# Experts sorted by token count, 24 small ones four at a time, and rows by one-hot products in the last 12 steps of a mixture-of-experts kernel

## What is computed

```
t = x.reshape(-1, D)                                    # 264 tokens, D = 1024
scores = sigmoid(t @ w_router)                          # 64 experts
biased = scores + router_bias                           # 8 groups of 8: the 4 best groups stay,
_, eidx = top_k(where(emask > 0, biased, -inf), 8)      # of them each token takes 8 experts
w = take_along_axis(scores, eidx);  w = w / sum(w) * 2.5
h = silu(t @ w_gate[e]) * (t @ w_up[e])                 # 1024 -> 256, for each expert
routed = (h * comb[..., e]) @ w_down[e]                 # 256 -> 1024, summed over experts
shared = (silu(t @ ws_gate) * (t @ ws_up)) @ ws_down    # one more expert for all tokens
x = layer_norm(ALPHA * x + routed + shared)
```

## Time and profile before

| | |
|---|---|
| median of the runs | 824.3 us (3 runs, 824.23 to 824.31) |
| the profiled execution: its time | 824.56 us |
| its span | 822.8 us |
| TensorE busy | 805.0 us, 98% |
| VectorE busy | 465.1 us, 57% |
| ScalarE busy | 166.1 us, 20% |
| GpSimd busy | 93.1 us, 11% |
| bytes moved by DMA | 262.15 MB |

### The profile page before, as it was taken

One profiled execution on the slowest core, in us unless ns is written; L12 is line 12 of the kernel. 1 busy time (PEld: TensorE's weight loads), 2 busy tenths in 40 slices (PEclk: granted clock), 3 DMA queues, 4 the chain that ended last, 5 costly groups with the idle time before them and its releaser, 6 DMA issues.

```text
span 822.8 us, 11931 instructions
## 1 busy us (share of the span) xinstructions
PE 805.0 (98%) x4283; PEld 500.9 (61%) x4283; DVE 465.1 (57%) x1178; ACT 166.1 (20%) x275; POOL 93.1 (11%) x105
## 2 busy tenths in 40 slices
PE   9999999999999999999999999999999999999995
PEld 7876788888788888544545445454544445445443
DVE  6989899999741367533434334443444434334356
ACT  2210112111221005321211212121121212112126
POOL 1119700000010002100000000000000000000021
PEclk9999999999999999999999999999999999999998
DMA  9432344445489946699999999999999999999981
GB/s 333 151 128 103 122 139 149 155 154 115 142 321 417 414 182 249 219 397 416 423 423 420 423 425 424 422 427 420 425 425 423 424 426 424 420 424 419 419 351 53
DMA packets 45372, 262.15 MB, mean 319 GB/s; under 512 B 9928, under 2 KB 10696, under 8 KB 26256
## 3 DMA queue, kind: packets, MB, share of 16 engines
q1 hardware_dynamic: 40720, 252.88, 76.6%
q0 software_dynamic: 4608, 8.66, 2.8%
HBM read 267.10 MB, written 2.53 MB: 328 GB/s over the span
## 4 chain that ended last, share of the span: by engine, by line
PE 83%; DMA 9%; SPq 6%; DVE 1%; issue 1%; ACT 1%; ACTq 0%; DVEq 0%
PE banks L1263 35%; PE banks L1474 21%; PE banks L1518 10%; PE banks L1435 6%; DMA high<-w_gu 5%; SPq L464 4%; DMA ring<-w_gu 4%; PE banks L1410 3%; SPq L472 2%; PE banks L1364 1%; PE banks L1278 1%; PE banks L1495 1%; PE banks L1290 1%; PE banks L1440 1%; DMA ring<-w_front 1%
## 5 line engine op out<-in xcount | busy, mean ns | idle before, releaser
L1474 PE MATMUL banks<-high,low 128*64 128x512 f32 x848 | 230.1, 593 | 0.9 <-DMA high<-w_gu 0.9
L1263 PE MATMUL banks<-xT,ring 128*128 128x264 f32 x768 | 176.3, 389 | 0.3 <-DMA ring<-w_front 0.3
L1170 DVE TENSOR_TENSOR cgb<-cgb,banks 128x264 f32<-128x264 f32 x248 | 89.8, 423 | 132.1 <-PE banks L1435 131.9
L1263 PEld LDWEIGHTS banks<-xT,ring 128*128 128x128 f32 x768 | 144.5, 190 | 30.4 <-issue 5.5
L1474 PEld LDWEIGHTS banks<-high,low 128*64 128x64 f32 x848 | 73.6, 137 | 138.6 <-issue 135.1
L1222 DVE SCALAR_TENSOR_TENSOR y_pair<-banks,sml,y_pair 128x1024 fp32r<-128x1024 f32 x31 | 39.8, 1284 | 121.8 <-ACT y_pair L725 121.8
L1474 PE MATMUL banks<-ring,low 128*64 128x512 f32 x176 | 77.6, 593 | 3.0 <-DMA ring<-w_gu 3.0
L562 POOL DMA_INDIRECT low<-x_rows_dram,idx x32 | 31.9, 997 | 423.5 <-DVE idx L1114 403.0
L1435 PEld LDWEIGHTS banks<-sw,y_pair 128*128 128x128 f32 x496 | 63.0, 188 | 24.9 <-issue 23.5
L1518 PE MATMUL banks<-high,mu 128*64 128x512 f32 x336 | 77.0, 599 | 0.7 <-ACT mu L705 0.7
L1435 PE MATMUL banks<-sw,y_pair 128*128 128x264 f32 x496 | 71.1, 293 | 0.0
(11 more groups left out here) (300 smaller groups left out, 859.9 us busy)
## 6 DMA issues: line engine op xcount, KB each, us to landing
high<-w_gu SPq DMA_DIRECT2D x35, 2048.0 KB, 24.0
high<-w_dn SPq DMA_DIRECT2D x40, 1024.0 KB, 21.9
ring<-w_front SPq DMA_DIRECT2D x78, 512.0 KB, 3.2
high<-w_gu SPq DMA_DIRECT2D x34, 1024.0 KB, 11.5
ring<-w_gu SPq DMA_DIRECT2D x7, 2048.0 KB, 28.8
us<-w_dn SPq DMA_DIRECT2D x11, 1024.0 KB, 21.8
ring<-w_gu SPq DMA_DIRECT2D x8, 1024.0 KB, 12.0
bgb<-w_dn SPq DMA_DIRECT2D x6, 1024.0 KB, 21.4
```

The costliest lines, as they stand in the source:

```text
L1170: dve.tensor_tensor(acc[:, n], acc[:, n], psum[:, bank, 0:T], ALU.add).then_inc(added, 1)
L1263: ins = pe.matmul(psum[:, 6 + n % 2, 0:T], ring[:, n % RING, k], rhs[:, k], start=(k == 0), stop=(k == KC - 1))
L1474: ins = pe.matmul(psum[SL * j:SL * j + SL, GU_BANK, :], xg[:, k, SL * j:SL * j + SL], gu[slots[j]][:, k], start=(k == 0), stop=(k == KC - 1))
```

## The change

It touches the expert part alone.

- **Order.** The first 8 experts keep their places. The other 56 are ranked by their number of tokens, on VectorE and TensorE, in front of and during step 0: a key for each expert, its rank by comparison, a permutation matrix `places`, and products that permute picks and gates (`turn_gates`, `sort_gates`, `count_sorted`, in the gate/up products of step 0). The expert numbers by place go into a tile `order`, from which SP reads each number into a register (`expert`) before it refills.
- **Four at a time.** Places 30 to 61 hold the 24 smallest experts in six groups of four, with pairs of the largest between them. Pairs 13 to 30 are worked off in 12 steps of `(1, 1, 2, 1, 2, 1), (2, 1, 2, 1, 2, 2)` pairs. A step of two pairs has 32 slots for each of its four experts, and its products go to four column parts of 32. It needs both pairs' weights, and both of its refills wait for its own `gu_done` and `dn_done`. There are 26 steps in place of 32.
- **Rows by products.** In the last 12 steps before the final one, `gather_rows` takes the place of the indirect DMA and of `turn`: 16 products of the token rows, which stay in SBUF (`xrow`, now in `xcb`, where `dn[7]` was), with `S32`, an f32 copy of the one-hot matrix that GpSimd makes (`widen`), and 8 small ones for the 8 sample rows. `dn[7]` and its early load go.
- The counts of rounds come from the sorted lists; rounds are added where one of the 24 smallest has more than 32 tokens or another more than 64. The three late refills are no longer in halves. The shared expert's down products move to the first three steps of four.

```diff
+        FIXED = 8
+        MIXED_FROM = 13
+        MIXED = ((1, 1, 2, 1, 2, 1), (2, 1, 2, 1, 2, 2))
+        mixed_pairs, nth = [], MIXED_FROM
+        for n in itertools.chain(*MIXED):
+            mixed_pairs.append(tuple(range(nth, nth + n)))
+            nth += n
...
+        SHARED_AT = {2: (0, 1, 2), 4: (3, 4), 6: (5, 6, 7)}
...
 
-        xrow = [y_flat[:, 0:D], y_flat[:, D:2 * D], y_rest]
+        xcb_flat = xcb[:].rearrange("p k t -> p (k t)")
+        xrow = [xcb_flat[:, 0:D], xcb_flat[:, D:2 * D], y_rest]
+        sample_rows = y_all[:, D + 64 - HC * P:D + 64]
+        S32, = carve(x_rows, (TC, 2 * SL))
...
-        DOWN_PAIRS = ((4, 5), (0, 1), (2, 3), (7, 5), (0, 1), (2, 3))
+        DOWN_PAIRS = ((4, 5), (0, 1), (2, 3))
...
-                sp.wait_ge(x1_scaled, KC)
-                sp.dma_start(dn[7], w_dn[6]).then_inc(dn_in[7], 16)
                 for c in range(TC):
                     sp.wait_ge(xrow_ready, c + 1)
...
+                def expert(place):
+                    return sp.value_load(order[0:1, bass.ds(place, 1)] if not isinstance(place, int) else order[0:1, place:place + 1], min_val=0, max_val=E - 1)
+
+                refill(0, 0, SLOT_PAIRS[0], DOWN_PAIRS[0], [6, 7], halves=True)
+                sp.wait_ge(order_ready, 1)
+                for it in range(1, 1 + PER_TURN):
+                    refill(it, it, SLOT_PAIRS[it % 3], DOWN_PAIRS[it % 3], [2 * it + 6, 2 * it + 7], halves=it < EARLY_HALVES, by_place=True)
+                    if it == 1:
+                        sp.wait_ge(weights_ready, 2)
+                        sp.wait_ge(rows_stored, 16 * TC)
+                        for g in range(2):
+                            sp.dma_start(sample_rows[32 * g:32 * g + NS], x_dram[LP:T, HC * P * g:HC * P * (g + 1)]).then_inc(rows_stored, 16)
                 sp.wait_ge(lists_ready, 1)
-                refills = sp.value_load(rounds[0:1, 1:2], min_val=TURNS - 1, max_val=MOST - 1)
-                for it in range(5):
-
-                    refill(it, SLOT_PAIRS[it % 3], DOWN_PAIRS[(it + 3) % 6] if it else (None, 5), [2 * it + 6, 2 * it + 7], halves=it < EARLY_HALVES)
...
+                after_middle = sp.value_load(rounds[0:1, 1:2], min_val=PLAIN - 2, max_val=MOST - 2)
+                middle = sp.snap(after_middle + 1)
+
+                def later_refill(q, it, step, fill):
+                    places = [(q * (2 * PER_TURN) + (2 * it + 6 + j)) % E for j in range(2)]
+                    fill(q * PER_TURN + it, q * PER_TURN + step, SLOT_PAIRS[it % 3], DOWN_PAIRS[it % 3], places, by_place=True)
+
+                with sp.Fori(0, middle) as q:
+                    for it in range(1 + PER_TURN, 1 + 2 * PER_TURN):
+                        later_refill(q, it, it, refill)
+                for a, pairs in enumerate(mixed_pairs):
+                    for it in pairs:
+                        if it + 3 < PAIRS:
+                            later_refill(after_middle, it, MIXED_FROM + a, last_refill if it + 3 == PAIRS - 1 else refill)
...
+                def widen(step, u):
+                    pool.wait_ge(select_ready, step + 1)
+                    pool.wait_ge(turned, step)
+                    pool.sem_inc(rows_moved, 1)
+                    pool.tensor_copy(S32, S[:, u]).then_inc(widened, 1)
...
+                for a in range(len(mixed_pairs)):
+                    widen(mixed * PER_TURN + (a + 2), a % 2)
...
+                def first_visit():
+                    match_tokens(0, 0)
+                    dve.wait_ge(weights_read, 4)
+                    dve.tensor_copy(gain[:, 0], meta[:, 0, 0:1]).then_inc(gain_ready, 1)
+                    dve.wait_ge(selected, 1)
+                    dve.wait_ge(shifted, 2)
+                    select(0, 4, 2, 3)
+                    dve.wait_ge(sort_products, GATES_SORTED)
+                    do(dve.tensor_scalar(order[0:1], psum[0:1, SORT_BANKS[1], TC * P:TC * P + E], 1.0, -1.0, ALU.mult, ALU.add))
+                    dve.sem_inc(order_ready, 1)
+                    do(dve.tensor_copy(sorted_gates, psum[:, SORT_BANKS[1], 0:TC * P].rearrange("p (c t e) -> p c t e", c=TC, t=2)))
+                    do(dve.tensor_copy(pk, picks))
+                    dve.sem_inc(sort_inputs, 1)
+                    do(dve.tensor_scalar(picks, picks, -1000.0, 1000.0, ALU.mult, ALU.add))
+                    gate_rows(0)
+                    dve.wait_ge(selected, 3)
+                    dve.wait_ge(turned, 1)
+                    dve.wait_ge(sw_ready, 1)
+                    dve.wait_ge(gain_ready, 1)
+                    indices(0, 6, 2)
+                    count_leftovers()
+                    split_rows(0, 0)
+                    split_gates(sorted_gates[:, :, 1, FIXED:E], slice(FIXED, E))
+
...
+                def gather_rows():
+                    def columns(k):
+                        return psum[:, 2 + k // 4, (k % 4) * P:(k % 4) * P + P]
+
+                    for k in range(KC):
+                        for c in range(2):
+                            pe.matmul(columns(k), xrow[c][:, k * P:k * P + P], S32[:, c], start=(k % 4 == 0 and c == 0), stop=False)
+                    for h in range(HC):
+                        for g in range(2):
+                            rows = slice(32 * g, 32 * g + NS)
+                            ins = pe.matmul(columns(HC * g + h), sample_rows[rows, h * P:h * P + P], S32[rows, 2], start=False, stop=(h == HC - 1))
+                    ins.then_inc(turned, 1)
+
+                def turn_gates():
+                    pe.wait_ge(sort_inputs, GATES_READY)
+                    pe.wait_ge(shared_silu, 1)
+                    for c in range(TC):
+                        ins = pe.transpose(psum[:, SORT_BANKS[0], c * P:c * P + P], gates[:, c].rearrange("p t e -> p (t e)"), ident[:])
+                    ins.then_inc(sort_products, 1)
+
+                def sort_gates():
+                    pe.wait_ge(sort_inputs, GATES_COPIED)
+                    pe.wait_ge(sort_inputs, RANKED)
+                    pe.wait_ge(shared_h, FC)
...
                                 pe.wait_ge(gu_last_rows[j], 16)
-                            ins = pe.matmul(psum[SL * j:SL * j + SL, GU_BANK, :], xg[:, k, SL * j:SL * j + SL], gu[slots[j]][:, k],
+                            ins = pe.matmul(psum[size * j:size * j + size, GU_BANK, :], xg[:, k, size * j:size * j + size], gu[s][:, k],
                                             start=(k == 0), stop=(k == KC - 1))
                         if k == HC - 1:
                             ins.then_inc(gu_mid, 1)
-                            if gathers is None:
+                            if last:
                                 pe.wait_ge(y_split, it)
                                 pe.wait_ge(sw_ready, it)
                                 combine(1 - u, before, shared, rows_summed_first=True)
+                        if before is None and k == 1:
+                            turn_gates()
+                        if before is None and k == 4:
+                            sort_gates()
                     ins.then_inc(gu_done, 1)
-
-                    if gathers is None:
+                    if before is None:
+                        count_sorted()
...
+                        if isinstance(before, int) and before == 0:
+                            pe.wait_ge(lists_ready, 1)
                         combine(1 - u, before, shared)
...
+                        if wide is None:
+                            pe.wait_ge(gathered[1 - u], gathers)
+                        else:
+                            pe.wait_ge(widened, wide)
                         if before is not None:
                             banks_added(before, 2, 3)
-                        turn()
-
+                        if wide is None:
+                            turn()
+                        else:
+                            gather_rows()
...
-                visit(turns * PER_TURN + 1, 1, SLOT_PAIRS[1], DOWN_PAIRS[1], turns * 32 + 16, 4, before=turns * (PER_TURN * KC))
+                        visit(q * PER_TURN + k, k % 2, [k], [q * 32 + 16 * (k // 3 + 1)], before=q * (PER_TURN * KC) + KC * (k - 1),
+                              ahead=((q * PER_TURN + (k + 2)) % PAIRS * 2, 2), gathers=q * 48 + 16 * ((k + 1) // 2 + 1))
+                pe.wait_ge(rows_stored, 16 * (TC + 2))
+
+                def mixed_place(a):
+                    pairs = mixed_pairs[a] if a < len(mixed_pairs) else (PAIRS - 1 + a - len(mixed_pairs),)
+                    return within((mixed * (2 * PER_TURN) + (2 + 2 * (pairs[0] - MIXED_FROM))) % E, len(pairs)), 2 * len(pairs)
+
+                for a, pairs in enumerate(mixed_pairs):
+                    loaded = [mixed * 32 + 16 * ((1 + r - MIXED_FROM) // 3 + 1) for r in pairs]
+                    visit(mixed * PER_TURN + (a + 1), (a + 1) % 2, pairs, loaded, before=mixed * (PER_TURN * KC) + KC * a, ahead=mixed_place(a + 2),
+                          wide=mixed * PER_TURN + (a + 2), shared=SHARED_AT.get(a, ()))
```

(57 more changed lines are left out.)

325 lines of the change are left out of this document (210 added, 115 removed).

## The result

The changed kernel takes 826.9 us (median of 8 runs, 825.7 to 828.1) against 824.2 for the kernel before on the same chip: ratio 1.003, 95% interval 1.0022 to 1.0039, so 1.8 to 3.2 us slower. A repeat on another occasion gave 827.0 (10 runs), ratio 1.003 again. The forecast was 823.4, slightly faster; the time lies inside the range given and on the other side of no change.

A forecast was written before the change was run, and what follows sets the result against it. The end was taken as pair 30's landing plus TensorE's work after it, so DMA bytes and idle time bound. Landing -10.4, after it +9.5, together -0.9: 823.7 profiled, 823.4 as median; 8 in 10 within 818.8 to 828.0.

The forecast's parts named there:

- landing of pair 30: Arrival of pair 30's gate/up weights, the last that TensorE waits for: 10.4 us earlier than 782.22, near 772.
- row products: Token rows made by products on TensorE in late steps: 5.3 us in place of 1.06 for turning.
- The gathers: In the weight stream, 1173 rows no longer gathered: -12.0 us, between 12.8 by q0's packet time and 11.3 by bytes.
- The early `w_dn`: Expert 6's down weights, loaded after step 0's down products in the full stream instead of early: +1.8 us (1.3 to 2.5).
- The front: Sort in front and in step 0, mostly hidden: net +0.3 us on the stream (-0.7 to +3).
- Loading whole instead of by halves: Three late pairs load whole, at 424 rather than 419 GB/s: -0.5 us (0 to -1).
- its +7.6: TensorE's work after pair 30's landing, now in a quad: 18.4 us where 10.8 was, +7.6 (6.5 to 8.7).
- The clock: Last quad after its wait: an idle engine is put at half rate, penalty certain, +1.9 us.
- Four tiles side by side: Gate/up of four experts takes 6.9 us; the rival, only two tiles at a time, gives 841 us, chance 5%.
- the stream has no hole in the quads: Weight loads during quads: 12 us still queued when the rest of the refills comes, so the stream never runs dry.
- The sort delays step 0: Slower rival, 12%: extra VectorE work before step 1's `sw` idles the DMA; ten slower operations give 826 to 827.5.
- The last quad is not slowed: Faster rival, 20%: clock stays up or recovers at once, row products at 0.213, gathers worth packet time: 819 us.

The follow-up runs named there:

- the 3 us experiment: The changed kernel with 12 more idle products (3.1 us) in step 0, behind the sort's products: 828.83 us, ratio 1.0056 to the kernel before.
- the gathers kept: The changed kernel with its quads, but the rows of all steps by gather and turn: 834.96 us, ratio 1.0131 to the kernel before.
- no quads: The changed kernel with its 18 late pairs one at a time, rows by products in all of them: 889.8 us (one run).
- the 36 idle products: The changed kernel with 36 products that nobody reads ahead of the last quad, while TensorE waits: 824.58 us, ratio 1.0003 to the kernel before.
- the kernel with halves: The changed kernel with pair 30's gate/up weights in halves, the last quad waiting for the second only at its middle: 821.12 us, ratio 0.9961.
- 28 idle products: The changed kernel with 28 products that nobody reads ahead of the last quad: 825.48 us, ratio 1.0013 to the kernel before.
- the kernel with both changes and 12 idle products: The changed kernel with pair 30's gate/up in halves, the last step's rows by gather and turn, and 12 idle products before the last quad: 818.38 us, ratio 0.9927.

## Why the prediction came out on the wrong side

The mechanism was right: the bound, the terms, their signs, the places. The sizes were not: the result differs from -0.9 by 3.4 us because the landing was forecast 1.7 to 2.3 us too early, the clock's part was in the repeat 0.7 too small, and 0.7 us at the end were in no term. Row products that came out 0.5 cheaper than predicted hide a part of this. The sum as predicted, and as two profiles of the changed kernel have it:

| term, us | predicted | first profile | repeat |
|---|---|---|---|
| landing of pair 30 | 771.8 | 773.45 | 774.06 |
| gate/up of the last quad, clock included | 8.85 | 8.77 | 9.64 |
| combine and transposes | 2.47 | 2.48 | 2.48 |
| row products | 5.3 | 4.83 | 4.83 |
| small transposes, down | 3.7 | 3.82 | 3.82 |
| from the last step's start to the end of the span | 29.8 | 30.05 | 30.07 |
| outside the span | 1.76 | 2.27 | 2.22 |
| sum | 823.7 | 825.7 | 827.1 |

*Landing, the step that failed first* (+1.7 and +2.3 us). The change was to move it by -10.4 and moved it by -8.8 and -8.2. By bytes moved up to it, read in narrow windows, the changed kernel needs 4.46 MB less than before, 10.5 us at 424 GB/s. The gathers were put at -12.0, between packet time and bytes, and the bytes (11.3) would have been the value to take; 0.16 MB more of instruction fetches (q8 and its like: 0.78 MB against 0.62) and some 0.2 MB of other loads that came ahead of pair 30 take another 0.8. The early `w_dn` was right: 1.8 predicted, and in the kernel before without it 1.8 by bytes and 1.6 by time. The front was put at +0.3 and is 0.3 to 0.4 MB, 0.7 to 1.0 us: I let step 0 begin 0.5 us sooner because the last cast is shorter, and it did not; and I costed TensorE's own 1.3 us (step 1 in truth starts 2.0 later) as mostly covered, where the 3 us experiment shows that only some 0.3 of each us is. Loading whole instead of by halves: -0.5 predicted, and the stream did move 0.27 MB more in 380 to 760 us, 0.6 us. Together these are -10.5 + 1.8 + 0.7 to 1.0 - 0.6, or -8.6 to -8.3. But what was given up with the halves in the last quad is 5.7 us by experiment. The prediction counted 3.3 for it inside its +7.6 (6.95 of gate/up behind the landing instead of 3.65); with halves the quad also starts on a load that lands 4.7 us sooner.

*The clock* was put at +1.9 from the start-up rows and measured 1.7, 2.6 and 2.8 in three profiles (gate/up 8.77, 9.64, 9.84 over the warm 7.05), 2.2 by the experiment that takes it away. The mechanism is as forecast; -0.2 to +0.9 is size. That the penalty is certain holds for the last quad of every kernel here without idle products (8.56 to 9.84), but not for waits of that length as such: two middle quads of the repeat stayed at 1.00 after 3.6 and 3.8 us.

*The end.* 0.25 in the last 30 us and 0.45 outside the span were in no term. The latter shows in all nine kernels with both quads and row products (2.2 to 2.3) and in none of the four others (1.76 to 1.80 in the profiled executions: before, before without the early load, the gathers kept, no quads); why, I can't say.

*Quads.* Four tiles side by side: the first quad's gate/up takes 7.00 us, the warm pace predicted from the SSM rows, so that rival falls. That the stream has no hole in the quads was right, as was the place of the waits; their size was not. The middle quads wait 3 to 5 us each (3 to 9 predicted), the first one not at all, and the last one 2.8 and 3.9 with six instructions between, where 9 to 11 were predicted; 22.7 in total. "89 us of steps are taken out of TensorE and all but 1 us of that becomes waiting" does not follow from the prediction's own lengths: 18 late steps of 14.05 are 253 us, six quads and six singles of 18.5 and 18.4 are 221. TensorE's busy time fell by 18.8 us (805.0 to 786.2). The sum does not use that figure.

*Rivals.* "The sort delays step 0" came half true, by TensorE's share of it (step 1 starts 2.0 us later), not by VectorE's queue. "The last quad is not slowed" is what the 36 idle products build: 824.6, no gain over the kernel before. It would have needed cheap rows too.

## What to carry to other kernels

When weights stream at a rate that nothing interrupts, find the last load that TensorE waits for and write down what still has to be computed when it has landed: a change that shortens the stream and lengthens that tail trades one for the other one to one, and merging two late steps into one makes the tail longer by the part that could have run on half the data. So merge and replace gathers in the middle, and keep the load in pieces and the rows by gather at the end (819.2 against 826.9). Whether the last two pairs should better stay unmerged was not tried. And count bytes by bytes, with a us of delay in front of the stream as most of a us at its end.

## What had not been expected of the hardware

The clock can fall after short pauses. In the kernel with halves TensorE stood for 1.48 and 1.44 us with 1.05 us of products between, and 0.53 was granted in 768 to 770 us; with 28 idle products, 3.25 us of standing were enough for 0.61 and 0.54. But the length of a pause does not decide it alone. In the kernel before, 2.16 us in front of the landing left the clock at 1.00:

```profile
782.22 0.64 PE L1474 MATMUL banks<-ring,low 128*64 128x512 f32 x1 [2.16 <-DMA ring<-w_gu]
```

So did 1.98 and 1.26 us in the kernel with both changes and 12 idle products, and 3.61 and 3.82 us in front of two middle quads of the repeat, where the same quads of the first profile were slow after 3.85 and 3.06. What decides between them stays open.

The time to come back varies too: 8.77, 9.64 and 9.84 us for the same instructions in three profiles. Those 1.1 us and the landing, which varies by 1.9, are of the size of the spread between executions (825.7 to 828.5 for the changed kernel). Idle products spent in the wait keep the clock up, and no price of them shows, if they reach up to the landing: the 36 ended at 772.75, and the last weights were there 0.6 us later.
